# Where the 31-tap convolution's running sums stand, and which engines form them

## The chip, the cores and the metric

The kernel is one program on 1 core of a Trainium2 chip. The metric is device time in microseconds (us). The kernel before took 2305.56 us, the median of three runs (2305.15 to 2306.09). Lower is better.

## The reference, cut to what matters

The program computes two transformer blocks for one sequence of 1024 tokens of width 1024, in float32. The change touches the first block alone, and there the part that follows the first projection:

```python
def conformer_conv(u, conv_dw, conv_dw_b, conv_ln_g, conv_ln_b, w_conv_pw):
    a, gate = jnp.split(u, 2, axis=-1)
    h = a * jax.nn.sigmoid(gate)
    h = lax.conv_general_dilated(                     # depthwise, causal, 31 taps, 512 channels
        h, conv_dw[:, None, :], window_strides=(1,), padding=[(30, 0)],
        dimension_numbers=("NWC", "WIO", "NWC"), feature_group_count=512) + conv_dw_b
    h = jax.nn.silu(layer_norm(h, conv_ln_g, conv_ln_b))
    return h @ w_conv_pw

proj = rms_norm(x) @ w_in                             # q, k, v, and u for the convolution
attn_out = sliding_window_attention(q, k, v, ...)     # window 128, 8 query heads
mixed = concatenate([attn_out, conv_out]) @ w_out
```

The 512 channels of the convolution are four blocks of 128 channels, one partition for each channel, with the 1024 tokens along the free dimension. A tap multiplies a shifted row of tokens by one number for each channel and adds it to a running sum: 31 taps for each block.

## The kernel before, in words

Every engine runs an instruction list written out by hand, in order, and waits on semaphores. `Port.wait_ge` is such a wait, and `then_inc(*signal.up(key))` raises a signal. A matmul of the reference is three on TensorE (`mm3`, L494): a high part of each operand and a low part, `wh`/`wl` for weights and `ah`/`al` for rows. ScalarE makes the high part of a weight chunk (`send_to`, L450) and VectorE or GpSimd the low part (`low_half`, L460). Five ring places hold the chunks, so `send_to(n)` waits until TensorE has done with chunk n - 5 (`ring_free`, L392).

The stages at the head of the program are these.

- *u units* (`mixer1_pe`, L1120). For channel block c and half th of the tokens TensorE forms two groups of 24 matmuls, i = 0 the gate (chunk 2c) and i = 1 the value (chunk 2c + 1). ScalarE takes the sigmoid of the gate (`gate`, L1272), and VectorE multiplies both into `hp` (`glu`, L1354). The PSUM bank of a unit comes from `u_bank` (L1069); `claim` (L488) makes TensorE wait until the bank's last user is done. The first half of the tokens for blocks 0 and 1 comes first, then the second half for blocks 0 and 1, then the small `tables` matmuls (L1101), then blocks 2 and 3.
- *kvq units*: keys, values and four query chunks, two groups each. ScalarE copies them out of PSUM (`kv_copy`, L1315).
- *swa* (`swa_pe`, L1510, and its partners): sliding-window attention in 32 steps. Step i takes `scores` on TensorE, row minima on VectorE (`maxima`, L1713), exponentials on ScalarE (L1638), a normalisation on GpSimd (L1787), transposes and the product with the values on TensorE. Keys and values of the memory (`mem_key`, `mem_value`) are formed between the steps 13 and 20. From step 21 on TensorE turns the finished convolution (`conv_turn`, L1559).

The convolution's taps are VectorE's, all four blocks of them, and are dealt out between its other duties by `some_taps` (L1255). Block 0 takes one `scalar_tensor_tensor` for each tap (`one_tap`, L1240), over 512 or 1024 tokens. Blocks 1 to 3 keep even and odd tokens apart and need 50 instructions of 512 columns in place of 62 (`split_op`, L1193): running sums over even taps (16 of them) and over odd taps (15), three that join them, and 16 with summed taps. The running sums stand in SBUF: `acc` and three tiles `odd_taps`. Two blocks' lists are mixed one by one (`in_turn`). What is not done before swa begins is dealt out in the steps 12 to 20 (`TAPS_AT`, L1456). GpSimd has nothing to do with the convolution, and from 29 us to 147 us of the span it only clears `kp` (L1438).

Of the kernel before, what the change touches and what calls it, by code (L numbers as in the profile page):

```python
# [11 lines left out]
ALU = mybir.AluOpType  # L12
# [226 lines left out]
def build(nc, ctx, I, out_dram):  # L239
# [42 lines left out]
    def landing(name):  # L282
# [9 lines left out]
    su = signal(DV, "dve_weight_sums")  # L292
    nr = signal(PL, "pool_normalised")
# [14 lines left out]
               *l_x0, l_cw, l_last, *l_sk, *l_out, *l_ff, *l_raw, *l_t2, *l_xd, su, nr]  # L308
# [640 lines left out]
    def rows_end_dve(ps, free=()):  # L949
# [26 lines left out]
        sb(f"s1_{i}", [128, 2, 257], off["extra"] + 10592 + 2080 * (i - 2)) for i in (2, 3)]  # L976
# [7 lines left out]
    odd_taps = {c: sb(f"odd_taps{c}", [128, 513], off["extra"] + 2080 * i) for i, c in enumerate(SPLIT)}  # L984
    tap_sums = sb("tap_sums", [128, 4, 16], off["extra"] + 2080 * len(SPLIT))
# [134 lines left out]
    def mixer1_pe():  # L1120
        e = PE.e
        turn_unit_matrix(16)
        x_turn_pe(0)
        turn_unit_matrix(8)
        x_turn_pe(1)
        turn_unit_matrix(12)
        u_quarter(0, 0)
        x_turn_pe(2)
        x_turn_pe(3)
        u_quarter(1, 0)  # L1130
        u_quarter(0, 1)
# [12 lines left out]
        for c in range(2):  # L1144
            for i in range(2):
                u_unit(c, i, 1)
        tables_pe()
        PE.ends("u0")
        for c in range(2, 4):
            for th in range(2):  # L1150
                for i in range(2):
                    u_unit(c, i, th)
        c = first["kvq"]
        for i, name in enumerate(KVQ):
            for th in range(2):
                columns_group(name, 0, th, c + i, KVQ_BANKS[name][th], (cp, (name, th)), rows_of("x", th))
            if name == "q0":
                for g in range(2):
                    claim(2 + g, cp, ("v1", g))
                    for th in range(2):  # L1160
                        PE.wait_ge(cp, ("v", th))
                    for j in range(4):
                        t = 4 * g + j
                        ins = e.transpose(P[:, 2 + g, 128 * j:128 * j + 128], v1t[:, 128 * t:128 * t + 128], ident[:, :])
                    ins.then_inc(*tp.up(("v1", g)))
        PE.ends("q3")
# [4 lines left out]
    taps, last_tap, split_last = [], {}, {}  # L1171
# [9 lines left out]
    def split_ops(c):  # L1181

        return in_turn([("even", c, j) for j in range(16)], [("odd", c, j) for j in range(1, 16)]) + [
            (name, c, 0) for name in ("both", "rows", "first")] + [("sum", c, j) for j in range(16)]

    def add_taps(c):
        if c in SPLIT:
            taps[:] = in_turn(taps, split_ops(c))
        else:
            taps[:] = in_turn(taps, [(c, w, 512, 1024) for w in range(FIRST_HALVES)] + [  # L1190
                (c, w, 0, 1024) for w in range(FIRST_HALVES, TAPS)])

    def split_op(name, c, j):  # L1193
# [3 lines left out]
        t_odd, bias = odd_taps[c], cwt[:, c, 31:32]  # L1197

        def behind(*names):
            for n in names:  # L1200
                if (n, c) in split_last:
                    DV.wait_ge(tap, split_last[n, c])

        if j == (1 if name == "odd" else 0) and name in ("even", "odd"):
            for th in range(2):
                DV.wait_ge(ev, ("u", c, th))
            DV.wait_ge(ev, "cwt")
            DV.wait_ge(zf, "hp")
        if name == "even":
            w = cwt[:, c, 2 * j:2 * j + 1]  # L1210
            if j == 0:
                ins = e.tensor_scalar(y_even, x_even[:, 0:512], w, None, ALU.mult)
            else:
                behind("even")
                ins = e.scalar_tensor_tensor(y_even, x_even[:, j:j + 512], w, y_even, ALU.mult, ALU.add)
        elif name == "odd":
            w, src = cwt[:, c, 2 * j - 1:2 * j], x_odd[:, j - 1:j + 512]
            if j == 1:
                ins = e.tensor_scalar(t_odd[:, :], src, w, None, ALU.mult)
            else:  # L1220
                behind("odd")
                ins = e.scalar_tensor_tensor(t_odd[:, :], src, w, t_odd[:, :], ALU.mult, ALU.add)
        elif name == "both":
            behind("even", "odd")
            ins = e.scalar_tensor_tensor(y_odd, y_even, bias, t_odd[:, 1:513], ALU.subtract, ALU.add)
        elif name == "rows":
            behind("even")
            ins = e.tensor_tensor(x_even, x_even, x_odd, ALU.add)
        elif name == "first":
            behind("both")  # L1230
            ins = e.scalar_tensor_tensor(y_even, y_even, bias, t_odd[:, 0:512], ALU.add, ALU.add)
        else:
            behind("both", "rows", "sum")
            DV.wait_ge(tap, "tap_sums")
            ins = e.scalar_tensor_tensor(y_odd, x_even[:, j:j + 512], tap_sums[:, c, j:j + 1], y_odd, ALU.mult,  # L1235
                                         ALU.add if j else ALU.subtract)
        ins.then_inc(*tap.up((name, c, j)))
        split_last[name, c] = (name, c, j)

    def one_tap(c, w, a, b):  # L1240
        e = DV.e
        src, dst = hp[:, c, w + a:w + b], acc[:, c, a:b]
        key = (c, w) if b - a == 1024 else (c, w, a)
        if w == 0:
            for th in range(a // 512, b // 512):
                DV.wait_ge(ev, ("u", c, th))
            DV.wait_ge(ev, "cwt")
            DV.wait_ge(zf, "hp")
            e.tensor_scalar(dst, src, cwt[:, c, 0:1], cwt[:, c, 31:32], ALU.mult, ALU.add).then_inc(*tap.up(key))
        else:  # L1250
            DV.wait_ge(tap, last_tap[c])
            e.scalar_tensor_tensor(dst, src, cwt[:, c, w:w + 1], dst, ALU.mult, ALU.add).then_inc(*tap.up(key))
        last_tap[c] = key

    def some_taps(halves):  # L1255

        while taps and halves > 0:
            op = taps.pop(0)
            if len(op) == 3:
                split_op(*op)  # L1260
                halves -= 1.1
            else:
                one_tap(*op)
                halves -= (op[3] - op[2]) // 512

    def mixer1_act():
        e = AC.e

# [3 lines left out]
        def gate(c, th):  # L1272
            AC.wait_ge(mm, (("u", c), 0, th))
            if c:
                AC.wait_ge(ev, ("u", c - 1, th))
# [23 lines left out]
        hi(7)  # L1299
        gate(1, 0)  # L1300
        gate(0, 1)
        send_to(5)
        gate(1, 1)
        send_to(6)
        AC.ends("u0")
        for c in range(2, 4):
            for th in range(2):
# [3 lines left out]
                send_to(2 * c + 3 + th)  # L1311
        c = first["kvq"]
# [17 lines left out]
        for i, name in enumerate(KVQ):  # L1330
            for th in range(2):
                kv_copy(name, th)
                if th == 0:
                    send_to(c + i + 3)
            if name == "q0":
                for g in range(2):
                    AC.wait_ge(tp, ("v1", g))
                    e.activation(v1[:, 4 * g:4 * g + 4, :], P[:, 2 + g, :].rearrange("p (t d) -> p t d", t=4),
# [3 lines left out]
    def mixer1_dve():  # L1342
        e = DV.e
        del taps[:]
        split_last.clear()
# [48 lines left out]
        taps.extend((0, w, 0, 512) for w in range(FIRST_HALVES))  # L1394
# [31 lines left out]
    def mixer1_pool():  # L1426
# [6 lines left out]
        PL.ends("u0")  # L1433
        after(PL, "u0")
        for g in range(2):
# [3 lines left out]
        ins.then_inc(*pz.up("kp1"))  # L1439
        PL.ends("q3")  # L1440
# [15 lines left out]
    TAPS_AT = {12: 2, 13: 3, 14: 4, **dict.fromkeys(range(15, 21), 5)}  # L1456
# [53 lines left out]
    def swa_pe():  # L1510
        e = PE.e

# [46 lines left out]
        def conv_turn(tb):  # L1559
            b = SWA_BANK["yc", tb]  # L1560
            claim(b, cp, ("yc", tb))
            for c in range(4):
                PE.wait_ge(tap, ("sum", c, 15) if c in SPLIT else (c, TAPS - 1))
# [131 lines left out]
    def swa_dve():  # L1695
# [41 lines left out]

        for i in range(N1 + 4):
# [29 lines left out]
            some_taps(2 * len(taps) if i == max(TAPS_AT) else TAPS_AT.get(i, 0))  # L1768
# [8 lines left out]
    def swa_pool():  # L1777
# [16 lines left out]
        PL.wait_ge(pz, "kp1")  # L1794
# [2716 lines left out]
```

## Time and profile before

| | before |
|---|---|
| median of three runs | 2305.56 us |
| the profiled execution's own time | 2305.78 us |
| its span | 2304.0 us |
| TensorE matmul busy | 2279.3 us (99%) |
| VectorE busy | 1399.7 us (61%) |
| ScalarE busy | 973.3 us (42%) |
| GpSimd busy | 918.8 us (40%) |

The span is the time from the first to the last instruction of one execution, and the execution's own time is 1.8 us longer. Busy shares are averages over the whole program. The change lies in the first 250 us, so the reader has to look at that stretch by itself. Start-to-start distances are what counts for a busy engine: the durations of neighbouring VectorE instructions overlap by some 0.08 us.

### The profile page before, as it was taken

What the parts mean: (1) busy time and instruction counts of PE and PEld (TensorE: products, weight loads), DVE (VectorE), ACT (ScalarE), POOL (GpSimd) and SP (SyncE); (2) the same over time, 40 slices, a digit from 0 to 9 for tenths busy, and PEclk for the clock granted to TensorE, in tenths of its full rate; (3) what the DMA queues carried; (4) which work ended last, traced back from release to release, by engine and by line L of the source; (5) the groups of instructions that cost most, each with busy time, mean ns of one, the idle gap of its engine ahead of it and who ended that gap; (6) DMA issues with size and microseconds to landing.
All of it is one profiled execution on the core that took longest, in us unless ns stands there. A gap on an engine that the chain in (4) does not pass through costs nothing.

```text
span 2304.0 us, 30846 instructions
## 1 busy us (share of the span) xinstructions
PE 2279.3 (99%) x11604; PEld 1904.6 (83%) x11604; DVE 1399.7 (61%) x2229; ACT 973.3 (42%) x1980; POOL 918.8 (40%) x813
## 2 busy tenths in 40 slices
PE   9999899999999999999999999999999999999998
PEld 8787688888888888888898878888888888888887
DVE  7999715945444477776533676154594444447776
ACT  4126734433232344455634765135443323234543
POOL 2014535488787700033112032221448878770003
PEclk9999999999999999999999999999999999999999
DMA  5222134233233368665002001243223323336865
GB/s 160 53 64 79 51 102 146 65 119 119 87 120 105 126 241 289 209 217 136 19 11 71 24 10 37 69 169 110 101 68 107 124 86 126 104 120 247 294 213 191
DMA packets 219590, 275.85 MB, mean 120 GB/s; under 512 B 17260, under 2 KB 144973, under 8 KB 216627
## 3 DMA queue, kind: packets, MB, share of 16 engines
q1 hardware_dynamic: 200594, 210.31, 29.3%
q10 hardware_dynamic: 18848, 63.58, 7.0%
q8 instruction: 92, 1.51, 0.3%
q14 instruction: 56, 0.45, 0.1%
HBM read 205.27 MB, written 68.57 MB: 119 GB/s over the span
## 4 chain that ended last, share of the span: by engine, by line
PE 92%; DVE 3%; ACT 2%; issue 1%; POOL 1%; DMA 0%; POOLq 0%; DVEq 0%; ACTq 0%
PE P L497 27%; PE P L499 27%; PE P L498 27%; PE P L3159 3%; PE P L3178 2%; PE P L3194 2%; PE P L509 1%; PE P L3116 1%; DVE acc L1235 1%; PE P L793 0%; DVE s L1725 0%; ACT p L3257 0%; DVE stats L3327 0%; PE P L1522 0%; POOL stats L572 0%
## 5 line engine op out<-in xcount | busy, mean ns | idle before, releaser
L497 PE MATMUL P<-ah,wh 128*128 128x512 f32 (+1 forms) x1136 | 441.4, 389 | 0.6 <-ACT go L2503 0.5
L499 PE MATMUL P<-ah,wl 128*128 128x512 f32 (+1 forms) x1136 | 438.9, 386 | 0.0
L498 PE MATMUL P<-al,wh 128*128 128x512 f32 (+1 forms) x1136 | 438.7, 386 | 0.0
L497 PE MATMUL P<-wh,ah 128*128 128x512 f32 (+2 forms) x1128 | 426.0, 378 | 0.0
L499 PE MATMUL P<-wh,al 128*128 128x512 f32 (+2 forms) x1128 | 423.4, 375 | 0.0
L498 PE MATMUL P<-wl,ah 128*128 128x512 f32 (+2 forms) x1128 | 423.0, 375 | 0.0
L579 POOL TENSOR_TENSOR stats<-stats,epsc 128x1 f32<-128x1 f32 x78 | 32.0, 411 | 647.6 <-ACT xn L2005 421.0
L497 PEld LDWEIGHTS P<-ah,wh 128*128 128x128 f32 x1136 | 213.5, 188 | 43.7 <-ACT go L2503 0.8
L499 PEld LDWEIGHTS P<-ah,wl 128*128 128x128 f32 x1136 | 213.4, 188 | 43.1
L498 PEld LDWEIGHTS P<-al,wh 128*128 128x128 f32 x1136 | 213.5, 188 | 42.2
L499 PEld LDWEIGHTS P<-wh,al 128*128 128x128 f32 x1128 | 212.2, 188 | 37.2
L497 PEld LDWEIGHTS P<-wh,ah 128*128 128x128 f32 x1128 | 212.3, 188 | 36.4 <-issue 0.3
L498 PEld LDWEIGHTS P<-wl,ah 128*128 128x128 f32 x1128 | 212.4, 188 | 36.0
L2960 POOL TENSOR_TENSOR wl<-ws,wh 128x512 fp32r<-128x512 f32 x154 | 203.8, 1345 | 3.1
L2960 POOL TENSOR_TENSOR wl<-stage,wh 128x512 fp32r<-128x512 f32 x128 | 181.5, 1433 | 48.4 <-DVE al L527 33.1
L463 POOL TENSOR_TENSOR wl<-stage,wh 128x1024 fp32r<-128x1024 f32 (+3 forms) x43 | 99.1, 2309 | 219.2 <-ACT wh L457 218.2
L2490 ACT ACTIVATE wh<-ws 128x512 fp32r<-128x512 f32 x160 | 96.5, 627 | 193.9 <-POOL ws L2953 189.5
L2643 ACT ACTIVATE ah<-rf 128x512 fp32r<-128x512 f32 x154 | 95.7, 621 | 64.3 <-DMA rf<-ff_rows 62.3
L2851 DVE TENSOR_TENSOR al<-rf,ah 128x512 fp32r<-128x512 f32 x154 | 105.2, 683 | 20.1 <-ACT ah L2643 20.0
L457 ACT ACTIVATE wh<-stage 128x1024 fp32r<-128x1024 f32 (+2 forms) x68 | 68.9, 1016 | 78.0 <-PE P L499 48.6
L2490 ACT ACTIVATE wh<-stage 128x512 fp32r<-128x512 f32 x132 | 79.7, 621 | 40.5 <-PE P L499 25.4
L2953 POOL TENSOR_TENSOR ws<-stage,ws 128x512 f32<-128x512 f32 x38 | 49.9, 1313 | 113.7 <-PE P L499 113.7
(384 smaller groups left out, 4377.4 us busy)
## 6 DMA issues: line engine op xcount, KB each, us to landing
rf<-ff_rows SPq DMA_DIRECT2D x154, 256.0 KB, 5.2
stage<-in_w_down_dram SPq DMA_DIRECT2D x110, 256.0 KB, 3.8
ff_rows<-sb ACTq DMA_DIRECT2D x22, 1024.0 KB, 5.0
stage<-in_w_gu_dram SPq DMA_DIRECT2D x44, 512.0 KB, 5.1
stage<-in_w_in_dram SPq DMA_DIRECT2D x22, 512.0 KB, 4.0
stage<-in_w_gate_dram SPq DMA_DIRECT2D x22, 512.0 KB, 4.1
stage<-in_w_up_dram SPq DMA_DIRECT2D x22, 512.0 KB, 5.1
ff_rows<-uo ACTq DMA_DIRECT2D x22, 512.0 KB, 3.0
```

Source lines behind the costliest of these rows:

```text
L457: e.activation(WH[n % RING][:, 0:plan[n][0]], stage[place(n)][:, 0:plan[n][0]], ACT.Copy).then_inc(*wh.up(n))
L463: port.e.tensor_tensor(WL[n % RING][:, 0:w], stage[place(n)][:, 0:w], WH[n % RING][:, 0:w].bitcast(F32), ALU.subtract).then_inc(*sig.up(n))
L497: e.matmul(out, lh, rh, start=start, stop=False, skip_group_check=onto)
L498: e.matmul(out, lh, rl, start=False, stop=False, skip_group_check=onto)
L499: return e.matmul(out, ll, rh, start=False, stop=stop, skip_group_check=onto)
L2490: AC.e.activation(hi, src, ACT.Copy).then_inc(*wh.up((self.name, (m, op))))
L2643: AC.e.activation(self.rows_place(u)[0], RF[b][:, :], ACT.Copy).then_inc(*ah.up((self.name, "split", u)))
L2851: DV.e.tensor_tensor(lo, RF[self.row_buffer(u)[0]][:, :], hi.bitcast(F32), ALU.subtract).then_inc(*al.up((self.name, "split", u)))
L2953: PL.e.tensor_tensor(self.halves(m, op)[2], a, b, sign).then_inc(*ws.up((self.name, (m, op))))
L2960: PL.e.tensor_tensor(lo, src, hi.bitcast(F32), ALU.subtract).then_inc(*wl.up((self.name, (m, op))))
L3159: ins = e.matmul(P[:, p[w // size], 0:n], self.q(h, i), part, start=y == 0, stop=y == len(keys) - 1)
L3178: ins = e.transpose(P[:, b, 128 * j:128 * j + 128], self.probs[x % 3][:, 128 * (g + j):128 * (g + j) + 128], ident[:, :])
```

## The change

Blocks 1, 2 and 3 remain with VectorE, but their two running sums stand in PSUM banks 2 and 3, which are taken from TensorE until swa begins. The blocks follow one another, since they share the two banks, and each takes 52 instructions. All of them come before the first `maxima` of swa. Block 0 is taken from VectorE: ScalarE forms each product of 512 columns into one of two buffers, and GpSimd adds it to `acc`, for 31 taps and two halves of the tokens. The second half of block 1 now comes ahead of that of block 0, and the banks of the u and kvq units are dealt out anew.

```diff
     def u_bank(c, i, th):
-        return (((0, 1), (4, 5)), ((6, 7), (0, 1)), ((4, 5), (6, 7)), ((0, 1), (2, 3)))[c][th][i]
-    TABLE_BANKS = (2, 3, 6)
-    FIRST_HALVES = 23
+        return (((0, 1), (4, 5)), ((6, 7), (0, 1)), ((4, 5), (6, 7)), ((0, 1), (4, 5)))[c][th][i]
+    TABLE_BANKS = (6, 7, 0)
+    GATE_AFTER = {(1, 0): 0, (2, 0): 1, (3, 0): 2, (0, 1): 1, (2, 1): 0, (3, 1): 2}
-    KVQ_BANKS = {"k": (4, 5), "v": (6, 7), "q0": (0, 1), "q1": (4, 5), "q2": (6, 7), "q3": (2, 3)}
+    KVQ_BANKS = {"k": (6, 7), "v": (0, 1), "q0": (4, 5), "q1": (6, 7), "q2": (0, 1), "q3": (4, 5)}
+    TAP_BANKS = (2, 3)
...
     def mixer1_pe():
-        for c in range(2):
+        for c in (1, 0):
             for i in range(2):
                 u_unit(c, i, 1)
         tables_pe()
...
     def add_taps(c):
+        taps.extend(in_turn([("even", c, j) for j in range(16)], [("odd", c, j) for j in range(1, 16)]) + [
+            (name, c, 0) for name in ("rows", "edge", "first", "both")] + [("sum", c, j) for j in range(16)] + [("out", c, 0)])
...
     def split_tap(name, c, j):
+        even, odd = (P[:, b, :] for b in TAP_BANKS)
+            if c - 1 in SPLIT:
+                DV.wait_ge(tap, ("out", c - 1, 0))
-                ins = e.scalar_tensor_tensor(y_even, x_even[:, j:j + 512], w, y_even, ALU.mult, ALU.add)
+                ins = e.scalar_tensor_tensor(even, x_even[:, j:j + 512], w, even, ALU.mult, ALU.add)
-                ins = e.scalar_tensor_tensor(t_odd[:, :], src, w, t_odd[:, :], ALU.mult, ALU.add)
+                ins = e.scalar_tensor_tensor(y_odd if j == 15 else odd, src, w, odd, ALU.mult, ALU.add)
+        elif name == "sum":
+            part = (odd, even)[j % 2]
+            if j >= 2:
+                DV.wait_ge(tap, ("sum", c, j - 2))
+            if j == 1:
+                ins = e.tensor_scalar(part, x_even[:, 1:513], w, None, ALU.mult)
+            else:
+                ins = e.scalar_tensor_tensor(y_odd if j == 14 else part, x_even[:, j:j + 512], w, part, ALU.mult,
+                                             ALU.add if j else ALU.subtract)
         else:
+            behind("sum")
+            ins = e.tensor_tensor(y_odd, even, y_odd, ALU.add)
...
+    def some_products(n):
+        while products and n > 0:
+            th, w = products.pop(0)
+            if w == 0:
+                AC.wait_ge(ev, ("u", 0, th))
+                AC.e.activation(acc[:, 0, tap_columns(th)], hp[:, 0, tap_columns(th)], ACT.Identity, bias=cwt[:, 0, 31:32],
+                                scale=cwt[:, 0, 0:1]).then_inc(*ep.up((th, 0)))
+            else:
+                k = 30 * th + w - 1
+                if k >= 2:
+                    AC.wait_ge(pt, (k - 2) // 30 * 100 + (k - 2) % 30 + 1)
+                AC.e.activation(tap_products[k % 2][:, :], hp[:, 0, tap_columns(th, w)], ACT.Copy,
+                                scale=cwt[:, 0, w:w + 1]).then_inc(*ep.up((th, w)))
+            n -= 1
+    def pool_tap(th, w):
+        PL.wait_ge(ep, (th, w))
+        if w > 1:
+            PL.wait_ge(pt, 100 * th + w - 1)
+        PL.e.tensor_tensor(acc[:, 0, tap_columns(th)], acc[:, 0, tap_columns(th)],
+                           tap_products[(30 * th + w - 1) % 2][:, :], ALU.add).then_inc(*pt.up(100 * th + w))
...
     def mixer1_act():
         hi(7)
+        products.extend((th, w) for th in range(2) for w in range(TAPS))
+        some_products(4)
         gate(1, 0)
+        some_products(7)
+        gate(1, 1)
+        send_to(5)
+        some_products(8)
         gate(0, 1)
-        send_to(5)
-        gate(1, 1)
         send_to(6)
         for c in range(2, 4):
             for th in range(2):
                 gate(c, th)
                 send_to(2 * c + 3 + th)
+                some_products(8)
         for i, name in enumerate(KVQ):
             for th in range(2):
                 kv_copy(name, th)
+                some_products(4)
...
     def mixer1_dve():
-        some_taps(6)
         lo(6)
         lo(7)
-        some_taps(3)
         glu(1, 0)
-        some_taps(FIRST_HALVES - 9)
+        glu(1, 1)
+        low_by_dve_to(5)
+        add_taps(1)
+        some_taps(12)
         glu(0, 1)
-        low_by_dve_to(5)
-        add_taps(0)
-        some_taps(14)
-        glu(1, 1)
         low_by_dve_to(6)
         tables_dve()
-        add_taps(1)
-        some_taps(6)
         for c in range(2, 4):
             for th in range(2):
-                some_taps(6)
+                some_taps(8)
                 glu(c, th)
                 low_by_dve_to(2 * c + 3 + th)
-                some_taps(8)
+                some_taps(5)
             add_taps(c)
         for i in range(6):
-            some_taps(16 if i < 5 else 6)
+            some_taps(15 if i < 5 else 12)
...
     def swa_dve():
+        some_taps(len(taps))
         for i in range(N1 + 4):
-            some_taps(2 * len(taps) if i == max(TAPS_AT) else TAPS_AT.get(i, 0))
```

## Rows read from the trace of the kernel before

**Rows 1.** The page: one line for each engine's busy time.
```profile
PE 2279.3 (99%) x11604; PEld 1904.6 (83%) x11604; DVE 1399.7 (61%) x2229; ACT 973.3 (42%) x1980; POOL 918.8 (40%) x813
```

**Rows 2.** Whole span, waits of TensorE: total us, times, longest.
```profile
PE P L497 <- DVE wl L463: 3.3, 1, 3.3
```

**Rows 3.** Timeline of swa, TensorE: start, us, instruction, [idle before, releaser].
```profile
234.88 0.50 PE L497 MATMUL P<-wh,mh 128*128 128x512 f32 x1 [3.32 <-DVE wl L463]
236.42 1.91 PE L1522 MATMUL P<-kp,q 128*128 128x256 f32 x4
239.97 1.13 PE L1522 MATMUL P<-kp,q 128*128 128x256 f32 x4
```

**Rows 4.** Windows of swa: busy us by engine, then granted clock, DMA.
```profile
230.00:240.00 10.00, 6.68 (x30) 4.79 (x28) 9.75 (x18) 2.77 (x7) 2.53 (x2) 0.83 0.09 28
236.00:238.00 2.00, 2.00 (x7) 1.53 (x6) 1.89 (x4) 0.60 (x1) 0.31 (x1) 0.57 0.47 139
```

**Rows 5.** Timeline of the u units, ScalarE and TensorE.
```profile
61.21 0.60 ACT L1276 ACTIVATE sg<-P 128x512 f32<-128x512 f32 x1 [9.33 <-PE P L499]
61.70 1.05 ACT L457 ACTIVATE wh<-stage 128x1024 fp32r<-128x1024 f32 x1
70.22 0.50 PE L497 MATMUL P<-ah,wh 128*128 128x512 f32 x1
108.67 0.60 ACT L1276 ACTIVATE sg<-P 128x512 f32<-128x512 f32 x1 [9.33 <-PE P L499]
```

**Rows 6.** Timeline from the u units to swa, VectorE.
```profile
72.54 0.15 DVE L1409 TENSOR_SCALAR nsink<-sinks 128x8 f32<-128x8 f32 x1
114.20 0.68 DVE L1358 TENSOR_TENSOR hp<-P,sg 128x512 f32<-128x512 f32 x1
114.80 1.21 DVE L463 TENSOR_TENSOR wl<-stage,wh 128x1024 fp32r<-128x1024 f32 x1
178.64 1.40 DVE L1235 SCALAR_TENSOR_TENSOR acc<-hp,tap_sums,acc 128x512 f32<-128x512 f32 x2
180.73 0.35 DVE L1725 CUSTOM_DVE_ANT_0 s<-P,b,nsink 128x128 f32<-128x128 f32 x1 [0.70 <-PE P L1522]
```

**Rows 7.** Timeline, VectorE: one chain of taps, a read of PSUM, alternating chains.
```profile
45.48 0.68 DVE L1358 TENSOR_TENSOR hp<-P,sg 128x512 f32<-128x512 f32 x1
46.09 10.98 DVE L1252 SCALAR_TENSOR_TENSOR acc<-hp,cwt,acc 128x512 f32<-128x512 f32 x14
107.57 1.41 DVE L1215 SCALAR_TENSOR_TENSOR acc<-hp,cwt,acc 128x512 f32<-128x512 f32 x2
110.22 1.40 DVE L1215 SCALAR_TENSOR_TENSOR acc<-hp,cwt,acc 128x512 f32<-128x512 f32 x2
```

**Rows 8.** Groups of VectorE by shape: busy, mean ns | idle before.
```profile
L4208 DVE MEMSET P<- 64x64 f32 x32 | 3.6, 112 | 1.8 <-ACT mv L4088 0.8 <-PE P L3159 0.7
L1381 DVE MEMSET hp<- 128x90 f32 x1 | 0.1, 133 | 0.0
L1380 DVE MEMSET hp<- 128x30 f32 x1 | 0.1, 83 | 0.0
```

**Rows 9.** Groups of GpSimd and ScalarE by shape.
```profile
L2953 POOL TENSOR_TENSOR es<-stage,es 128x512 f32<-128x512 f32 x4 | 5.2, 1291 | 0.0
L1845 ACT ACTIVATE zs<-P,cwt 128x512 f32<-128x512 f32 x8 | 6.2, 771 | 1.4 <-PE P L1834 1.4
```

**Rows 10.** Timeline of swa: GpSimd beside VectorE.
```profile
187.46 1.04 POOL L1791 TENSOR_TENSOR s<-s,stats 128x512 f32<-128x512 f32 x1 [0.51 <-DVE stats L1711]
187.93 0.48 DVE L1725 CUSTOM_DVE_ANT_0 s<-P,b,nsink 128x256 f32<-128x256 f32 x1 [0.56 <-PE P L1522]
233.78 1.94 POOL L1791 TENSOR_TENSOR s<-s,stats 128x512 f32<-128x512 f32 x1 [4.07 <-DVE stats L1711]
234.74 4.68 DVE L1235 SCALAR_TENSOR_TENSOR acc<-hp,tap_sums,acc 128x512 f32<-128x512 f32 x5
242.32 0.47 DVE L1725 CUSTOM_DVE_ANT_0 s<-P,b,nsink 128x256 f32<-128x256 f32 x1
```

More of the change, by code:

```diff
@@ L292, in build @@
     su = signal(DV, "dve_weight_sums")
+    ep = signal(AC, "act_tap_products")
+    pt = signal(PL, "pool_taps")
     nr = signal(PL, "pool_normalised")
@@ L975, in build @@
     s1 = [big(f"s1_{i}", [128, 2, 257], 76.5 + 2.5 * i) for i in range(2)] + [
-        sb(f"s1_{i}", [128, 2, 257], off["extra"] + 10592 + 2080 * (i - 2)) for i in (2, 3)]
+        sb(f"s1_{i}", [128, 2, 257], off["extra"] + 256 + 8 * KB + 2080 * (i - 2)) for i in (2, 3)]
     v1t = big("v1t", [128, 1024], 76.5)
@@ L983, in build @@
     SPLIT = (1, 2, 3)
-    odd_taps = {c: sb(f"odd_taps{c}", [128, 513], off["extra"] + 2080 * i) for i, c in enumerate(SPLIT)}
-    tap_sums = sb("tap_sums", [128, 4, 16], off["extra"] + 2080 * len(SPLIT))
+    tap_sums = sb("tap_sums", [128, 4, 16], off["extra"])
+    tap_products = [sb(f"tap_product{i}", [128, 512], off["extra"] + 256 + 2 * KB * i) for i in range(2)]
     def input_loads():
@@ L1163, in mixer1_pe @@
                         t = 4 * g + j
-                        ins = e.transpose(P[:, 2 + g, 128 * j:128 * j + 128], v1t[:, 128 * t:128 * t + 128], ident[:, :])
+                        ins = e.transpose(P[:, g, 128 * j:128 * j + 128], v1t[:, 128 * t:128 * t + 128], ident[:, :])
                     ins.then_inc(*tp.up(("v1", g)))
         PE.ends("q3")
-    taps, last_tap, split_last = [], {}, {}
+    taps, last_tap, products, pool_taps = [], {}, [], []
     def in_turn(first, second):
@@ L1179, in in_turn, with split_tap @@
         return mixed
-    def split_ops(c):
-        return in_turn([("even", c, j) for j in range(16)], [("odd", c, j) for j in range(1, 16)]) + [
-            (name, c, 0) for name in ("both", "rows", "first")] + [("sum", c, j) for j in range(16)]
     def add_taps(c):
[L1187 to L1193, printed above, removed]
+        taps.extend(in_turn([("even", c, j) for j in range(16)], [("odd", c, j) for j in range(1, 16)]) + [
+            (name, c, 0) for name in ("rows", "edge", "first", "both")] + [("sum", c, j) for j in range(16)] + [("out", c, 0)])
+    def split_tap(name, c, j):
         e = DV.e
         x_even, x_odd, y_even, y_odd = hp_split[:, c, 0, :], hp_split[:, c, 1, :], acc_split[:, c, 0, :], acc_split[:, c, 1, :]
-        t_odd, bias = odd_taps[c], cwt[:, c, 31:32]
+        even, odd = (P[:, b, :] for b in TAP_BANKS)
+        bias = cwt[:, c, 31:32]
         def behind(*names):
             for n in names:
-                if (n, c) in split_last:
-                    DV.wait_ge(tap, split_last[n, c])
-        if j == (1 if name == "odd" else 0) and name in ("even", "odd"):
+                if (n, c) in last_tap:
+                    DV.wait_ge(tap, last_tap[n, c])
+        if (name, j) in (("even", 0), ("odd", 1)):
             for th in range(2):
@@ L1211, in split_op @@
             if j == 0:
-                ins = e.tensor_scalar(y_even, x_even[:, 0:512], w, None, ALU.mult)
+                ins = e.tensor_scalar(even, x_even[:, 0:512], w, None, ALU.mult)
             else:
                 behind("even")
-                ins = e.scalar_tensor_tensor(y_even, x_even[:, j:j + 512], w, y_even, ALU.mult, ALU.add)
+                ins = e.scalar_tensor_tensor(even, x_even[:, j:j + 512], w, even, ALU.mult, ALU.add)
         elif name == "odd":
-            w, src = cwt[:, c, 2 * j - 1:2 * j], x_odd[:, j - 1:j + 512]
+            w, src = cwt[:, c, 2 * j - 1:2 * j], x_odd[:, j:j + 512]
@@ L1218, in split_op @@
             if j == 1:
-                ins = e.tensor_scalar(t_odd[:, :], src, w, None, ALU.mult)
+                ins = e.tensor_scalar(odd, src, w, None, ALU.mult)
             else:
                 behind("odd")
-                ins = e.scalar_tensor_tensor(t_odd[:, :], src, w, t_odd[:, :], ALU.mult, ALU.add)
-        elif name == "both":
[L1224 to L1231, printed above, removed]
-        else:
[L1233 to L1236, printed above, removed]
+                ins = e.scalar_tensor_tensor(y_odd if j == 15 else odd, src, w, odd, ALU.mult, ALU.add)
+        elif name == "rows":
+            behind("even", "odd")
+            ins = e.tensor_tensor(x_even, x_even, x_odd, ALU.add)
+        elif name == "edge":
+            ins = e.tensor_scalar(y_even[:, 0:1], even[:, 0:1], bias, None, ALU.add)
+        elif name == "first":
+            ins = e.scalar_tensor_tensor(y_even[:, 1:512], even[:, 1:512], bias, y_odd[:, 0:511], ALU.add, ALU.add)
+        elif name == "both":
+            ins = e.scalar_tensor_tensor(odd, even, bias, y_odd, ALU.subtract, ALU.add)
+        elif name == "sum":
+            part = (odd, even)[j % 2]
+            DV.wait_ge(tap, "tap_sums")
+            behind("both", "rows")
+            if j >= 2:
+                DV.wait_ge(tap, ("sum", c, j - 2))
+            w = tap_sums[:, c, j:j + 1]
+            if j == 1:
[3 more added lines that the diff above has]
+                                             ALU.add if j else ALU.subtract)
+        else:
+            behind("sum")
+            ins = e.tensor_tensor(y_odd, even, y_odd, ALU.add)
@@ L1237, in split_op @@
         ins.then_inc(*tap.up((name, c, j)))
[L1238 to L1261, printed above, removed]
-            else:
-                one_tap(*op)
-                halves -= (op[3] - op[2]) // 512
+        last_tap[name, c] = (name, c, j)
+    def some_taps(n):
+        while taps and n > 0:
+            split_tap(*taps.pop(0))
+            n -= 1
+    def tap_columns(th, w=0):
+        return slice(512 * th + w, 512 * th + w + 512)
@@ L1266, in mixer1_act @@
+    def pool_tap(th, w):
[4 more added lines that the diff above has]
+                           tap_products[(30 * th + w - 1) % 2][:, :], ALU.add).then_inc(*pt.up(100 * th + w))
     def mixer1_act():
         e = AC.e
+        del products[:]
         def hi(t):
@@ L1433, in mixer1_pool @@
         PL.ends("u0")
+        for th in range(2):
+            for w in range(1, TAPS):
+                pool_tap(th, w)
         after(PL, "u0")
+        PL.wait_ge(pt, 100 + TAPS - 1)
         for g in range(2):
@@ L1511, in swa_pe @@
         e = PE.e
+        for b in TAP_BANKS:
+            held[b] = (tap, ("out", SPLIT[-1], 0))
         def scores(i):
@@ L1562, in conv_turn @@
             for c in range(4):
-                PE.wait_ge(tap, ("sum", c, 15) if c in SPLIT else (c, TAPS - 1))
+                PE.wait_ge(*((tap, ("out", c, 0)) if c in SPLIT else (pt, 100 + TAPS - 1)))
             for c in range(4):
```

19 lines of the change are left out of this document (10 added, 9 removed).

## The prediction, made before the run

> **What bounds the kernel now.** I read the page first: TensorE is busy for 99% of the span [rows 1], so a change can give back only time in which TensorE stands still or runs slowly, and it costs whatever new standstill it makes. Then the waits of TensorE: the longest, 3.3 us, is for a weight's low part from VectorE [rows 2]. The timeline puts it in swa, with its end at 234.9 us, inside `mem_value` [rows 3]: VectorE is at the taps of the steps 12 to 20 and its low part comes late. The windows show VectorE 9.75 of 10 us busy there, and the granted clock at 0.57 in the windows just behind the standstill, so part of that time ran at the lower of the two levels, 1.2 GHz [rows 4]. The step from 236.42 to 239.97 us took 3.55 us; at 0.57 of the clock 0.43 of it, 1.5 us, was the clock's. So the taps in swa cost 3.3 + 1.5 = 4.8 us, and that is all there is to win: in the rest of the first 200 us TensorE hardly waits.
>
> **The part that brings something.** No tap is left in the steps of swa, so VectorE forms the low part behind its few duties of the step. What is late next is the weight's high part from ScalarE, which was there first even before. I take the whole 4.8 us as given back.
>
> **The gate of block 0, second half.** `send_to(5)` waits until TensorE is done with chunk 0. Before, that was the first of the four groups of the second half; with block 1 put first it is the third, which ended at 61.2 us [rows 5]. ScalarE is in order, so the chunk (1.05 us) is sent at 62.25, and the eight products and `gate(0, 1)` queue behind it. A product is 0.77 us, by the nearest row with a per-partition scale [rows 9]; an add of 128x512 on GpSimd 1.29 us [rows 9], say 1.30 with its semaphore. With two buffers the eighth product waits for the sixth add: 62.25 + 0.77 + 6 x 1.30 + 0.77 = 71.6, and the sigmoid (0.60) ends at 72.2. TensorE claims that bank for the first group of block 2, which it began at 70.22 [rows 5]. It now begins at 72.3: 2.1 us lost. Its ends: 0.5 us with adds of 1.04 us and 5.9 us with adds of 1.94 us, the shortest and the longest of the rows with an add of that size [rows 10].
>
> In the later rounds ScalarE needs 0.6 + 1.05 for gate and chunk and 9.3 for eight products, 10.95 us. TensorE takes (108.67 - 70.22) / 7 = 5.49 us for a group, 10.98 for a unit [rows 5]. That just fits; a gate may also come 5.4 us late before `glu` misses it. After 51 products eleven are left for the kvq units, hidden beside TensorE's groups, and GpSimd, idle before, is through by about 140 us; its `kp` fills come behind and are wanted at 182. All of that I cost at nothing. If an add took 1.94 us this cover would be gone (rival D).
>
> **VectorE's list up to swa.** Before the last `glu` of the u units 12 + 8 + 3 x 13 = 59 of the 156 tap instructions are dealt out. The price of an instruction in alternating chains is (110.22 - 107.57) / 4 = 0.66 us from start to start [rows 7], so 13 of them, a `glu` (0.60) and a low part (1.14) make 10.3 us, and VectorE keeps up with TensorE. Behind it stand 97 instructions, 6 low parts and the `glu`. Before, VectorE took from 114.20 to 180.04 us for one `glu`, six low parts and 89 tap instructions [rows 6]: (65.8 - 0.6 - 6.8) / 89 = 0.656 each. Now it begins at 114.2 + 2.1 = 116.3 and is through at 116.3 + 7.4 + 97 x 0.656 = 187.3 us. The low parts read two SBUF operands; beside an add each side can lose some 0.9 us (1.94 against 1.04 on GpSimd [rows 10]), and two or three of them still meet adds: 1.0 us more, 188.3. The first `maxima`, at 180.73 before [rows 6], could be at 182.8. It is 5.5 us late, and with it everything: TensorE can run two steps' scores and then has no bank.
>
> That rests on a price that no row has, an instruction of 512 columns whose running sum stands in PSUM. What rows show: a read of PSUM costs from start to start 46.09 - 45.48 = 0.61 us, less than a tap, and a fill of 64 columns in PSUM takes 112 ns, between the 83 ns of 30 columns and the 133 ns of 90 in SBUF [rows 7, 8]. So I take 0.656, the row nearest in kind. The ends: 0.61, with which the 97 are through 4.5 us earlier, and 0.784, the link of a chain in which each waits for the one before (10.98 / 14 [rows 7]), with which they are through 12.4 us later, and 1 us more is lost in the u units.
>
> The Trainium skill has a rule against this place (Perfetto Trace Analysis, Optimizing Scalar/DVE Operations): VectorE's fixed overhead is about 60 ns on SBUF and about 125 ns on PSUM. An estimate by that page adds 65 ns to each of the 97, 6.3 us, and the kernel would come at 2316. The rows on reads and on fills above do not bear it out.
>
> **The clock.** TensorE stands still for some 5 us when swa begins, longer than the 3.3 us behind which the clock was at 0.57 [rows 3, 4]. I price it as there, 1.5 us; its ends are 0 (the first steps are small matmuls that wait for others) and 3. Behind the 2.1 us of the gate I take none; at most another 1.5.
>
> **GpSimd and VectorE beside one another.** `maxima` reads one operand from PSUM and one from SBUF: 0.48 us with an add running beside it, 0.47 without, and the add takes 1.04 [rows 10]. Five taps with both operands in SBUF took 4.68 us with an add of 1.94 beside them. So taps with the sum in PSUM should leave the adds alone. The Trainium skill says the same (SBUF — State Buffer, Who interferes with whom): VectorE contends with GpSimd's reads when it has two SBUF inputs. If it were otherwise, rival D would hold.
>
> **The sum.** 2.1 (gate) + 5.5 (late start of swa) + 1.5 (clock) - 4.8 (taps out of swa) = +4.3 us. Made against the profiled execution, 2304.0 us of span and 1.8 around it, 2305.8: 2310.1. The median of the runs lies 0.2 below that execution: 2309.9 us.
>
> **Rivals.**
> - B, dearer sums: an instruction on PSUM costs about half of what lies between 0.656 and 0.784 more, 0.06. For it: they read and write the same bank, and no row shows that. Against it: the fill and the read of rows 7 and 8. 97 x 0.06 = 5.8: 2315.7 us; at the upper end 2323.
> - C, VectorE in time, so not slower: at 0.61 an instruction the lateness falls from 5.5 to 1.0 and the slow clock with it: 2.1 + 1.0 - 4.8 = -1.7, 2303.9 us. With short adds as well (gate 0.5) -3.3. It decides from 0.656 - 4.3 / 97 = 0.61 us an instruction downwards. For it: one operand less in SBUF, and a two-operand instruction that read PSUM had 0.61. Against it: the scalar operand is still read, and that is what sets a tap off from the 0.61.
> - D, GpSimd's chain the bound: adds of 1.94 us make a round 0.6 + 1.05 + 1.5 + 11.6 = 14.8 against 10.98. The gate costs 5.9, four rounds 3.8 each less the 5.4 that a gate may be late, 9.8; swa's start moves with them: +11 over the forecast, 2321 us. For it: the low parts do collide. Against it: only one of VectorE's 15 instructions in a unit does.
>
> **How the numbers follow.** My forecast has 0.50, C 0.25, B 0.17, D 0.08. A measurement of this kernel tells 0.2%, 4.6 us, from no change. The forecast, +4.3 with some 2 us either way, lies at that bound, half on each side: 0.25 same, 0.25 slower. C is 0.17 same and 0.08 faster (no standstill at the gate as well). With B and D slower has 0.50, same 0.42, faster 0.08. The range runs from 2302.5 (C with short adds) to 2318 (B and a part of its upper end).
>
> **What would show it.** Right: `gate(0, 1)` at 71.6 and TensorE idle for about 2 us until it ends; VectorE without a gap from some 84 us until 188; the first `maxima` there, TensorE idle for about 5 us ahead of the third scores, and a low granted clock behind it; no wait for a low part in `mem_value`. The tap instructions' distance decides between the forecast, B and C; GpSimd's mean add decides D. I am wrong if swa begins at 183 us, or if swa is no shorter than before from its first `maxima` on.

## The result, and the profile after

The kernel after took 2313.54 us, the median of 7 runs (2312.29 to 2314.45), against 2305.32 us for 7 runs of the kernel before: a ratio of 1.0036, 95% interval 1.0024 to 1.0047. The forecast was 2309.9 us in 2302.5 to 2318; slower came about, and by 3.6 us more than forecast. The profiled execution's span went from 2304.0 to 2311.7 us.

TensorE's waits, longest first: total, times, longest us. The two shown are new and are its longest single waits, and the wait for VectorE's `wl` [rows 2] is gone.

```profile
PE P L1547 <- DVE stats L1750: 7.6, 1, 7.6
...
PE P L499 <- ACT sg L1295: 2.8, 1, 2.8
```

The gate, from the timeline of ScalarE, GpSimd and TensorE (start, length, engine, line, operation, count, idle time before). Each further product waits 0.7 us for an addition, and from the second on the additions follow at 1.41 to 1.44 us, not at the 1.30 taken from [rows 9]. The first stood beside VectorE's low part and took 1.72 us. TensorE goes on at 73.13 us where it had gone on at 70.22 [rows 5].

```profile
61.27 1.06 ACT L459 ACTIVATE wh<-stage 128x1024 fp32r<-128x1024 f32 x1 [7.10 <-PE P L501]
62.24 1.32 ACT L1273 ACTIVATE tap_product<-hp,cwt 128x512 f32<-128x512 f32 x2
...
71.87 0.72 ACT L1273 ACTIVATE tap_product<-hp,cwt 128x512 f32<-128x512 f32 x1 [0.69 <-POOL acc L1281]
72.50 0.58 ACT L1295 ACTIVATE sg<-P 128x512 f32<-128x512 f32 x1
...
63.02 11.67 POOL L1281 TENSOR_TENSOR acc<-acc,tap_product 128x512 f32<-128x512 f32 x8 [7.23 <-ACT tap_product L1273]
...
73.13 0.50 PE L499 MATMUL P<-ah,wh 128*128 128x512 f32 x1 [2.84 <-ACT sg L1295]
```

Windows of the kernel after: stretch, busy time of PE, PEld, DVE, ACT, POOL with counts, granted clock, DMA share, GB/s. The clock is at 0.72 of full behind the first standstill, a mean of both levels (0.66, 0.50 and 0.99 in the three windows of 2 us), and at 0.50, the lower level of 1.2 GHz, behind the second.

```profile
74.00:80.00 6.00, 6.00 (x21) 4.81 (x20) 5.94 (x10) 0.03 (x1) 0.70 (x1) 0.72 0.40 107
...
188.00:190.00 2.00, 0.00 (x0) 0.00 (x0) 2.00 (x4) 0.00 (x0) 0.00 (x0) 1.00 0.00 0
190.00:192.00 2.00, 0.00 (x0) 0.00 (x0) 2.00 (x4) 0.00 (x0) 0.00 (x0) 0.67 0.60 156
192.00:194.00 2.00, 0.45 (x2) 0.45 (x3) 1.97 (x10) 0.47 (x3) 0.00 (x0) 0.50 0.95 377
194.00:196.00 2.00, 2.00 (x11) 1.91 (x11) 1.24 (x11) 1.71 (x10) 1.14 (x3) 0.50 0.92 336
```

VectorE's timeline. The last tap in PSUM begins at 191.50 and the first `maxima` at 192.88 us, 12.1 later than the 180.73 of [rows 6]. Low parts take up to 1.8 us where additions run beside them and 1.21 where none does (180.49). At 147.22 VectorE had been idle 2.15 us for a chunk's high part. Twelve taps take 7.98 us and still stand 0.66 us apart.

```profile
119.08 0.68 DVE L1383 TENSOR_TENSOR hp<-P,sg 128x512 f32<-128x512 f32 x1
119.68 1.52 DVE L465 TENSOR_TENSOR wl<-stage,wh 128x1024 fp32r<-128x1024 f32 x1
...
147.22 1.60 DVE L465 TENSOR_TENSOR wl<-stage,wh 128x1024 fp32r<-128x1024 f32 x1 [2.15 <-ACT wh L459]
...
180.49 1.21 DVE L465 TENSOR_TENSOR wl<-stage,wh 128x1024 fp32r<-128x1024 f32 x1
...
182.94 7.98 DVE L1242 SCALAR_TENSOR_TENSOR P<-hp,tap_sums,P 128x512 f32<-128x512 f32 x12
...
191.50 0.74 DVE L1242 SCALAR_TENSOR_TENSOR P<-hp,tap_sums,P 128x512 f32<-128x512 f32 x1
```

That high part was late because ScalarE was. In ScalarE's timeline the chunk stands behind products that waited for GpSimd's additions:

```profile
143.45 0.72 ACT L1273 ACTIVATE tap_product<-hp,cwt 128x512 f32<-128x512 f32 x1 [0.79 <-POOL acc L1281]
144.90 0.72 ACT L1273 ACTIVATE tap_product<-hp,cwt 128x512 f32<-128x512 f32 x1 [0.72 <-POOL acc L1281]
145.64 0.60 ACT L1349 ACTIVATE v1t<-P 128x512 f32<-128x512 f32 x1
146.14 1.05 ACT L459 ACTIVATE wh<-stage 128x1024 fp32r<-128x1024 f32 x1
```

TensorE's timeline shows where the scores of the first two steps end and the third must wait. The first line is the same place in the kernel before:

```profile
180.09 1.05 PE L1522 MATMUL P<-kp,q 128*128 128x128 f32 x8
...
184.94 1.05 PE L1547 MATMUL P<-kp,q 128*128 128x128 f32 x8
193.55 2.08 PE L1547 MATMUL P<-kp,q 128*128 128x128 f32 x8 [7.56 <-DVE stats L1750]
```

The difference of the spans, 7.7 us, then reads: 2.9 standstill at the gate, 1.95 behind it (184.94 is 4.85 later than the 180.09 at which the scores began before; some 1.75 of it is the slow clock, and 0.2 a wait for `v1t`, ScalarE's copy of the values), 7.3 more until the first `maxima` (12.1 - 4.85), 0.9 clock behind that, 5.3 given back in the rest of swa. The sum is +7.75.

### The profile page after: what moved, and what is told of

Same layout as the page of the kernel before. It is cut to its first block, busy times and chain, and to the rows that moved or that the text cites. A ratio compares the mean times of both kernels' runs of the same rounds, so it can differ in the third digit from the quotient of the medians.

```text
span 2311.7 us, 30979 instructions
## 1 busy us (share of the span) xinstructions
PE 2280.4 (99%) x11604; PEld 1906.2 (82%) x11604; DVE 1361.4 (59%) x2181; ACT 1015.5 (44%) x2042; POOL 993.4 (43%) x873
## 4 chain that ended last, share of the span: by engine, by line
PE 89%; DVE 4%; ACT 3%; POOL 3%; issue 1%; DMA 0%; ACTq 0%; SPq 0%; POOLq 0%; DVEq 0%
PE P L499 26%; PE P L501 26%; PE P L500 26%; PE P L3183 3%; POOL acc L1281 2%; PE P L3202 2%; PE P L3218 2%; PE P L511 1%; PE P L3140 1%; PE P L1547 1%; DVE P L1242 1%; PE P L795 0%; ACT wh L459 0%; DVE P L1215 0%; PE P L1572 0%
## 5 line engine op out<-in xcount | busy, mean ns | idle before, releaser
L1281 POOL TENSOR_TENSOR acc<-acc,tap_product 128x512 f32<-128x512 f32 x60 | 83.7, 1395 | 38.7 <-ACT tap_product L1273 30.9
```

The lines of the kernel that those rows point to most:

```text
L1281: PL.e.tensor_tensor(acc[:, 0, tap_columns(th)], acc[:, 0, tap_columns(th)], tap_products[(30 * th + w - 1) % 2][:, :], ALU.add).then_inc( ...
```

## The experiments

All ran beside the kernel before, whose median was 2305.1 us for the first four, 2305.4 for the others.

**1. The gate ahead of the products.**

```diff
-        some_products(8)
         gate(0, 1)
         send_to(6)
+        some_products(8)
```

> The changed kernel with one thing moved: ScalarE takes the sigmoid of block 0's second half (and the chunk behind it) ahead of the eight products, not behind them. Queue theory: TensorE waited 2.84 us for that sigmoid and ran at a low clock behind it, so its last kvq group ended 4.85 us later than in the kernel before (184.94 against 180.09 us); both go, VectorE's list is anchored on TensorE's last u unit and moves along, so the kernel comes 4.9 us earlier, at 2308.7 us, and the first row minima of swa at about 188 us. Rival (VectorE's list alone is the bound): VectorE works through from 63.5 us and would be as late anyway; the wait goes, TensorE waits the same 4.9 us longer ahead of the third scores, and the time stays at 2313.5.

2314.0 us, ratio 1.0037 [1.0022, 1.0052]: nothing gained. That is the rival's time, but not by the rival's path. TensorE's waits show that the gate's is gone and another has come, for `v1t`, which ScalarE copies behind products that wait for additions:

```profile
PE P L1168 <- ACT v1t L1349: 5.1, 1, 5.1
PE P L1547 <- DVE stats L1750: 5.0, 1, 5.0
```

VectorE is hardly earlier at the last `glu` of the u units (118.21 us, and 119.08 in the kernel after), since it now waits there for ScalarE's sigmoid. It waits for the same chunk as in the kernel after, and from there to the first `maxima` its list is as long as ever (147.83 to 193.47 us, 45.64; in the kernel after 147.22 to 192.88, 45.66):

```profile
118.21 0.69 DVE L1383 TENSOR_TENSOR hp<-P,sg 128x512 f32<-128x512 f32 x1 [0.77 <-ACT sg L1295]
...
147.83 1.58 DVE L465 TENSOR_TENSOR wl<-stage,wh 128x1024 fp32r<-128x1024 f32 x1 [2.12 <-ACT wh L459]
...
193.47 0.34 DVE L1750 CUSTOM_DVE_ANT_0 s<-P,b,nsink 128x128 f32<-128x128 f32 x1
```

So the standstill at the gate was not a term of its own. Both it and the late chunk stand behind products that wait for additions; that these are the cause is tested in experiment 7.

**2. Fewer sums in block 3.** Left out are 12 of its 16 summed taps, and the waits between the rest are renumbered.

```diff
-[("sum", c, j) for j in range(16)]
+[("sum", c, j) for j in range(16) if not (c == 3 and 2 <= j < 14)]
```

> The changed kernel without 12 of the 16 summed taps of block 3 (j = 2 to 13 are left out, 7.9 us of VectorE's list at 0.656 us each). Queue theory: swa begins with its first row minima, which VectorE reached 7.3 us late; the wait of 7.56 us ahead of the third scores falls to 0.3 us or less, the low clock behind it (0.9 us) goes too, and the time is 2313.5 - 8.2 = 2305.3 us. Rival (the late start is made up later, because the first steps of swa wait on ScalarE and GpSimd anyway): less than 3 us gained, 2310.5 or more.

2305.26 us, ratio 1.000 [0.999, 1.0009]. It gave 8.3 us for 12 x 0.66 = 7.9 us less on VectorE, whose first `maxima` begin at 185.14 us in place of 192.88, and TensorE's wait of 7.6 us for them is down to 0.3. So the length of the list counts one for one once swa's start hangs on it, and the slow clock behind the wait (0.9 us) goes with it.

**3. The running sums in SBUF.** Two SBUF tiles take the place of the PSUM banks; the rest is as in the kernel after.

```diff
-        even, odd = (P[:, b, :] for b in TAP_BANKS)
+        even, odd = (t[:, :] for t in tap_parts)
```

> The changed kernel with VectorE's two running sums in SBUF tiles in place of the two PSUM banks; everything else is the same. Port theory: every tap now reads two SBUF operands and collides with GpSimd's adds. An add goes from 1.44 us (start to start) to near 2, a tap beside an add from 0.66 to 0.8 or more, ScalarE's gates come late by more than the 5.4 us allowed, and the time rises by 10 us or more, to 2324 or above. Rival (place does not matter, the adds are slow by themselves): 2313.5 us, adds and taps as before.

2352.29 us, ratio 1.0205 [1.0189, 1.022]: 38.8 us dearer than in PSUM. The first `maxima` begin at 231.45 us, 38.6 later than in PSUM. VectorE's timeline has the same instruction at 1.7 us while GpSimd adds (11.97 / 7), and at 0.67 once it is through, at 169.8 us (4.72 / 7). GpSimd's 31 additions in a row took 58.94 us instead of 47.77. Most of that difference is one addition: from 88.08 to 97.40 us it took 9.32 us, and VectorE's taps beside it stood 0.66 us apart, as if nothing ran there. The products, and with them the next sigmoid, waited for it, and VectorE then waited 8.05 us for that sigmoid:

```profile
118.69 11.97 DVE L1243 SCALAR_TENSOR_TENSOR tap_part<-hp,tap_sums,tap_part 128x512 f32<-128x512 f32 x7
...
187.87 4.72 DVE L1243 SCALAR_TENSOR_TENSOR tap_part<-hp,tap_sums,tap_part 128x512 f32<-128x512 f32 x7
...
88.08 58.94 POOL L1282 TENSOR_TENSOR acc<-acc,tap_product 128x512 f32<-128x512 f32 x31 [12.55 <-ACT tap_product L1274]
...
88.08 9.32 POOL L1282 TENSOR_TENSOR acc<-acc,tap_product 128x512 f32<-128x512 f32 x1 [12.55 <-ACT tap_product L1274]
...
88.88 0.73 DVE L1216 SCALAR_TENSOR_TENSOR tap_part<-hp,cwt,tap_part 128x512 f32<-128x512 f32 x1
89.54 0.73 DVE L1223 SCALAR_TENSOR_TENSOR tap_part<-hp,cwt,tap_part 128x512 f32<-128x512 f32 x1
...
106.14 0.69 DVE L1384 TENSOR_TENSOR hp<-P,sg 128x512 f32<-128x512 f32 x1 [8.05 <-ACT sg L1296]
```

**4. TensorE kept busy in the gap at the gate.** 14 transposes stand behind the tables.

```diff
         tables_pe()
+        PE.wait_ge(ev, ("u", 1, 1))
+        for _ in range(14):
+            e.transpose(P[:, 1, 0:128], ident[:, :], ident[:, :])
```

> The changed kernel with 14 more transposes of the unit matrix on TensorE right behind the table matmuls, in the time in which it waits for the sigmoid. Clock theory: the sigmoid comes at the same time, so TensorE begins block 2 at 73.1 us as before, but the granted clock of the window 74 to 80 us, 0.72 in the changed kernel, stays at 1.0: 1.9 us less, 2311.6 us. Rival (the time lost behind the gap is not the clock's): 2313.5 us or more.

2313.08 us, ratio 1.0034 [1.0022, 1.0046], 1.5 us above the clock theory's time. The clock stayed up:

```profile
74.00:80.00 6.00, 6.00 (x28) 4.93 (x28) 5.83 (x10) 0.14 (x1) 0.80 (x1) 1.00 0.39 105
```

The time did not follow: TensorE now waits 1.9 us for `v1t`, and the first `maxima` begin at 193.14 us. What TensorE gains ahead of the late start is lost in waiting for it.

**5. The kernel before, without its taps in swa.** Left out are the taps of steps 12 to 20 except the last sum of each block.

```diff
-            some_taps(2 * len(taps) if i == max(TAPS_AT) else TAPS_AT.get(i, 0))
+            if i == min(TAPS_AT):
+                taps[:] = [t for t in taps if t[0] == "sum" and t[2] == 15]
+                some_taps(2 * len(taps))
```

> The kernel before, with the 31 taps of swa left out except the last sum of each block (whose signal TensorE waits for): what the taps in swa cost, alone. My prediction's term: 3.3 us of standstill and 1.5 of clock go, 2305.1 - 4.8 = 2300.3 us; by the comparison of the two traces it is 5.3, 2299.8. Rival: another engine is late next in those steps (ScalarE's high part, or GpSimd's normalisation) and takes a part over: 2302 to 2304.

2299.99 us, ratio 0.9977 [0.9968, 0.9986]: 5.4 us, a little more than the 4.8 of the forecast.

**6. The first and the second together.**

> Gate of block 0 ahead of the products (as in the first experiment) and 12 summed taps of block 3 left out (as in the second), together. If the two losses simply add, as my prediction's sum had it, this gives 2305.3 - 2.8 - 1.95 = 2300.5 us. Rival, from the trace of the first: ScalarE is behind because each product waits for GpSimd's addition, and then keeps TensorE waiting 5.1 us for v1t instead, so the scores begin at about 188 us whatever VectorE does: 2305.3 + 3 = 2308 us, with the v1t wait at 5 us and no wait for the maxima.

2307.67 us, ratio 1.0009 [1.0, 1.0019], 2.4 us more than the second alone although the gate's standstill is gone. The wait for `v1t` heads the list, and none of any length for the maxima is left. ScalarE holds swa's start here: VectorE waits 3.1 us for the first scores, and these begin at 188.24 us, against 184.50 in the second.

```profile
PE P L1168 <- ACT v1t L1350: 5.2, 1, 5.2
```

**7. ScalarE's list alone.** On top of the first: products where ScalarE and GpSimd stood idle, and no more in a round than GpSimd can add meanwhile.

```diff
         gate(1, 1)
+        some_products(4)
         send_to(5)
         gate(0, 1)
+        some_products(3)
         send_to(6)
-        some_products(8)
+        some_products(4)
...
                 send_to(2 * c + 3 + th)
-                some_products(8)
+                some_products(7 if (c, th) != (3, 1) else 4)
...
-                some_products(4)
+                some_products(3)
```

> ScalarE's list alone, on top of the gate of block 0 first: 4 products ahead of send_to(5), 3 ahead of send_to(6), then 4; 7 in a round instead of 8, 4 in the last; 3 instead of 4 behind each copy of the kvq units. Theory (GpSimd's chain of additions paces ScalarE, which brings the weight's high part and v1t late): the waits for v1t (5.1 us) and of VectorE for the high part (2.1 and 0.8 us) go, TensorE is at the scores at about 183 us, VectorE at the first maxima 3 us earlier than 193.5, 2314.0 - 3 = 2311 us, with a wait for the maxima of 7 to 9 us in place of 5.0. Rival (VectorE's list has no slack of its own, the waits only displaced work): 2314 us.

2307.27 us, ratio 1.0008 [0.9998, 1.0017]: 6.7 us less than in the first, where 3 were expected. No wait for `v1t` or of VectorE for a high part is left behind 62.5 us, the last `glu` of the u units begins at 114.39 us instead of 118.21, and the first `maxima` at 186.98 instead of 193.47. TensorE is at the scores at 180.21 us, as before the change (180.09):

```profile
180.21 1.05 PE L1549 MATMUL P<-kp,q 128*128 128x128 f32 x8
187.66 2.07 PE L1549 MATMUL P<-kp,q 128*128 128x128 f32 x8 [6.39 <-DVE stats L1752]
```

The mechanism held, its size was taken too small: I had counted only the waits behind the last `glu`.

**8. VectorE's list too.** 8 taps fill the 5.8 us in which it waited for chunk 5, and blocks follow as soon as their halves are there.

```diff
         glu(1, 1)
+        add_taps(1)
+        some_taps(8)
         low_by_dve_to(5)
-        add_taps(1)
-        some_taps(12)
+        some_taps(5)
         glu(0, 1)
         low_by_dve_to(6)
+        some_taps(3)
         tables_dve()
...
-                some_taps(8)
+                some_taps(13 if (c, th) == (2, 0) else 8)
                 glu(c, th)
+                if th == 1:
+                    add_taps(c)
                 low_by_dve_to(2 * c + 3 + th)
-                some_taps(5)
-            add_taps(c)
+                some_taps(6)
...
-            some_taps(15 if i < 5 else 12)
+            some_taps(14 if i < 5 else len(taps))
```

> ScalarE's list as in the run before, and VectorE's: 8 taps of block 1 ahead of the low part of chunk 5 (where it stood idle 5.8 us), 16 ahead of the tables instead of 12, 13 ahead of the first glu of block 2 instead of 8, then 14 in a unit instead of 13, block after block as soon as its halves are there. Theory (the start of swa is all that the change costs, and it hangs on idle time in these two lists): VectorE is through by 178 to 182 us, TensorE goes on to the scores at 180.5 to 183 without a wait, and the taps out of swa count in full: 2305.1 - 4.8 + 0 to 1 = 2300.3 to 2301.5 us. Rival (what GpSimd's additions cost the low parts and ScalarE stays, 1.5 to 2 us for each of five): swa begins 4 to 5 us late as before, 2304 to 2306 us.

2303.42 us, ratio 0.999 [0.9981, 1.0], between the two theories. The first `maxima` begin at 182.40 us, 0.4 after the latest time that the theory allowed; TensorE waits 2.1 us, and the clock falls behind it:

```profile
183.07 1.65 PE L1552 MATMUL P<-kp,q 128*128 128x128 f32 x8 [2.11 <-DVE stats L1755]
...
184.00:186.00 2.00, 1.75 (x8) 1.39 (x7) 1.75 (x12) 1.90 (x10) 1.64 (x5) 0.50 0.95 324
186.00:188.00 2.00, 2.00 (x11) 1.28 (x10) 1.52 (x4) 1.20 (x6) 1.49 (x2) 0.70 0.93 346
```

**9. The last seven instructions in swa.** The sums 10 to 15 of block 3 and the joining addition stand in the steps 11 to 16, over SBUF; sums 8 and 9 carry the two parts over from PSUM.

```diff
+                late = (y_odd, tap_products[0][:, :])[j % 2]
+                out, part = (late, late if j > 9 else part) if c == 3 and j >= 8 else (y_odd if j == 14 else part, part)
...
-            some_taps(14 if i < 5 else len(taps))
+            some_taps(14 if i < 5 else len(taps) - 7)
...
-        some_taps(len(taps))
         for i in range(N1 + 4):
...
+            some_taps({11: 1, 12: 1, 13: 1, 14: 2, 15: 1, 16: 1}.get(i, 0))
```

> The kernel with both lists changed, and the last seven instructions of block 3's sums put in the steps 11 to 16 of swa, their running sums in SBUF (the PSUM banks come free with the ninth sum). In the kernel without it VectorE reaches the first maxima at 182.4 us and TensorE waits 2.1 us for it. Theory (that wait is all that is left of the late start, and VectorE has room in steps 11 to 16): seven times 0.66 = 4.6 us earlier, so no wait; 2303.4 - 2.1 = 2301.3 us, and up to 0.5 us less where the clock had fallen; the interval below 1 against the kernel before. Rival (taps in swa delay the maxima or a low part again, as the 31 of before did in mem_value): the 2.1 us come back there, 2303 to 2304 us.

2299.79 us, ratio 0.9977 [0.9968, 0.9986]: faster than both kernels, 1.5 us less than expected (why is open), and within 0.2 us of the fifth, which leaves work out. The first `maxima` wait for TensorE now, not it for them, and the clock stays at 1.00:

```profile
177.36 0.74 DVE L1246 SCALAR_TENSOR_TENSOR tap_product<-hp,tap_sums,P 128x512 f32<-128x512 f32 x1
180.86 0.35 DVE L1759 CUSTOM_DVE_ANT_0 s<-P,b,nsink 128x128 f32<-128x128 f32 x1 [2.76 <-PE P L1556]
...
182.00:184.00 2.00, 1.35 (x11) 1.15 (x10) 1.42 (x12) 2.00 (x12) 1.29 (x3) 1.00 0.93 272
```

## Why the prediction was nearly right, step by step

- **The price of a tap in PSUM**, the widest unknown: 0.66 us from start to start, as forecast, so rivals B and C fall. For a tap the trace does not bear out the dearer PSUM access of the Trainium skill (Perfetto Trace Analysis, Optimizing Scalar/DVE Operations): with the sums in SBUF and no addition beside them the distance was 0.66 to 0.67 too. The three instructions of a block that begin a sum (`TENSOR_SCALAR`) are dearer in PSUM, 0.66 us against 0.40.
- **The port.** That PSUM sums leave GpSimd alone held: beside them its additions took 1.27 to 1.30 us each. Experiment 3 shows what the other place costs, which also agrees with the Trainium skill's rule (SBUF — State Buffer, Who interferes with whom).
- **The gate**: +2.1 forecast, 2.9 measured, since additions are up to 1.44 us apart, not 1.30. The row I took [rows 9] was right for an addition alone, 1291 ns against 1.29 to 1.30 here. But 0.14 us lies between one and the next in a chain that waits for semaphores, where I had put 0.01, and an addition beside a low part takes 1.7 to 2.1 us; that is why the mean is 1395 ns (83.7 us for 60).
- **"10.95 us, that just fits"** is the step that failed. The gates of blocks 2 and 3 began at 80.98, 93.15, 104.13 and 116.45 us, 11.8 apart on average, where TensorE needs 10.9. My sum with 1.44 in place of 1.30 gives 11.8 too (0.6 + 1.05 + 2 x 0.77 + 6 x 1.44). The trace shows what sets the round: GpSimd adds from 83.21 to 130.98 us with some 0.14 us between one addition and the next, so a round of eight products is as long as eight additions, 8 x 1.44 = 11.5 us, and 0.8 longer where one stands beside VectorE's low part, as in the second line here. So two of the three distances are 12.2 and 12.3 us; the third, 11.0, holds seven additions.

```profile
84.65 1.29 POOL L1281 TENSOR_TENSOR acc<-acc,tap_product 128x512 f32<-128x512 f32 x1
87.52 2.09 POOL L1281 TENSOR_TENSOR acc<-acc,tap_product 128x512 f32<-128x512 f32 x1
```

ScalarE fell behind, so the copies and chunks of the kvq units, which I had costed at nothing, came late (the first copy of the keys began at 130.29 us, in experiment 7 at 119.67, where TensorE ran 4.7 us earlier), GpSimd was through at 152.8 us and not at 140, and VectorE waited 2.15 us at 147.22. It is rival D in a mild form: most additions were far from 1.94 us, but the cover was only 0.03 us thick. (D's own terms give (5.9 - 2.1) + 9.8 = 13.6 us over the forecast, not the 11 stated there; nothing hangs on it.)
- **VectorE's list**: forecast at the last `glu` of the u units at 116.3 and at the first `maxima` at 188.3; measured 119.08 and 192.88. Of the 4.6 us, 2.8 lie ahead of that `glu` (0.8 for the later gate, some 1.75 for the slow clock behind it, and the rest on VectorE itself, with low parts of 1.5 to 1.8 us). In experiment 1, without the first two, ScalarE's late sigmoid still held this `glu` until 118.21. The other 1.8 lie behind it, about the 2.15 us wait. So the late start was 7.3 instead of 5.5 beyond a TensorE that was itself 4.85 late.
- **The clock**: 1.5 forecast behind swa's start, 0.9 measured; none forecast behind the gate, some 1.75 measured.
- **Taps out of swa**: -4.8 forecast, -5.3 in the traces, -5.4 in experiment 5.
- **The form of the sum.** I added gate and late start. Experiment 1 took the gate's standstill and its clock away, experiment 4 the clock alone, and neither gained anything beyond the noise (+0.5 and -0.5 us), so these terms lay in the shadow of the late start: what counts is when the first `maxima` begin, 12.1 us late. In 7, 8 and 9, where they go together with what stood behind them, 13.7 us come back. The number itself was near partly by luck: the first `maxima` came 4.6 us later than forecast, and 1.1 of that is hidden by a cheaper clock behind them (0.6) and by taps in swa that had cost more than I took (0.5).

No run separates which part of ScalarE's lateness comes from the chain itself and which from the low parts that collide with it, but the trace allows an estimate. Against TensorE's 10.9 us a round of eight is 0.6 us too long by the chain (11.5) and another 0.8 by the one addition of 2.1 us beside a low part.

## What to carry to other kernels

When work goes to an idle engine through a second engine's queue, compare the slow one's pace with each round's length, and give a margin: whatever stands behind in the second queue runs at that pace. Standstills that lead up to one late start don't add; find the latest arrival and shorten that, then the next. And before work is taken out of a busy stage altogether, look for steps in it that have room: seven instructions there were worth 3.6 us.

## What the runs showed of the hardware that was not expected

- A VectorE instruction with both large operands in SBUF takes 1.7 us per 128x512 beside GpSimd's additions and 0.66 without them, and these additions then take 1.55 instead of 1.30 us each; the same with the running sum in PSUM takes 0.66 beside them and leaves them at 1.30. Once, in experiment 3, it went the other way: VectorE kept its 0.66 us over eleven taps, and one addition took 9.32 us.
- An instruction that reads one tile and no running sum (`TENSOR_SCALAR`, 128x512) took 0.40 us from start to start into SBUF (experiment 3, 183.02 to 183.42) and 0.66 into PSUM (kernel after, 182.28 to 182.94), both without additions beside it.
- A 2.8 us standstill of TensorE was followed by a clock of 0.72 over the next six microseconds, some 1.7 us lost. With 14 small transposes in the gap, which left 1.2 us of it, the clock stayed at 1.00. In experiment 8 a wait of 2.1 us at swa's start, among small matmuls, was followed by windows at 0.50 and 0.70.
